# Layer 1's mixer in a two-layer encoder: values before keys and queries, the norm and the gates inside projection phases

## What is computed

```python
hn = rms_norm(x, mix_norm[layer])
u = hn @ od_w_in[j]
# mlstm_mixer(u, ...):
qk, v, o, gates = jnp.split(u, [ML_QK_W, ML_QK_W + D_MODEL, ML_QK_W + 2 * D_MODEL], axis=-1)
qk = jax.nn.silu(centered_dwconv(qk, conv_w, conv_b))
...
hs = mlstm_chunkwise(jnp.concatenate([q, flip(q)], axis=1), jnp.concatenate([k, flip(k)], axis=1),
                     jnp.concatenate([v, flip(v)], axis=1), log_i, log_f)
...
return hsum * jax.nn.sigmoid(o)
```

## Time and profile before

| | us |
|---|---|
| median of 3 runs | 2720.84 (2719.23 to 2721.32) |
| profiled execution, its time | 2724.51 |
| profiled execution, its span | 2722.5 |
| the five phases: renorm | 1411.4 to 1440.6 |
| ml_project_qk | to 1559.4 |
| ml_project_vo | to 1753.5 |
| ml_gates | to 1798.1 |
| ml_scan | to about 1911 |

### The profile page before, as it was taken

How to read it: one execution, slowest core, us unless ns; L and a number is a source line. 1 busy time by engine, 2 the same in 40 slices (tenths; PEclk the granted TensorE clock), 3 DMA queues, 4 the chain that set the end, 5 groups by cost and what they waited for, 6 DMA issues and landing times. The chain is left out here.

```text
span 2722.5 us, 32997 instructions
## 1 busy us (share of the span) xinstructions
PE 2428.2 (89%) x11788; PEld 1995.0 (73%) x11788; DVE 1827.1 (67%) x2083; ACT 1452.7 (53%) x1776; POOL 483.5 (18%) x433
## 2 busy tenths in 40 slices
PE   5989989796959999999948999779695999999995
PEld 4768877585857888888836888667584888888882
DVE  5748856578358998899835301078546988888980
ACT  4337842322227887788834212146423778887870
POOL 0001100100002332333200000025200323332310
PEclk9999999897979999999978999979796999999997
DMA  4010011101339999999980101200424999999994
GB/s 171 31 64 1 1 39 42 70 31 36 117 115 344 389 385 381 382 389 391 373 327 22 50 31 64 91 1 1 144 109 170 387 367 380 369 387 380 395 375 167
DMA packets 85787, 542.51 MB, mean 199 GB/s; under 512 B 18870, under 2 KB 22551, under 8 KB 59704
## 3 DMA queue, kind: packets, MB, share of 16 engines
q1 hardware_dynamic: 64232, 503.11, 47.0%
q0 software_dynamic: 19008, 33.61, 5.1%
q10 hardware_dynamic: 2448, 4.46, 0.4%
HBM read 521.70 MB, written 55.05 MB: 212 GB/s over the span
## 5 line engine op out<-in xcount | busy, mean ns | idle before, releaser
L2119 DVE TENSOR_TENSOR wL<-ring,wH 128x2048 fp32r<-128x2048 f32 x384 | 869.1, 2288 | 153.7 <-ACT wH L2066 148.4
L2066 ACT CAST wH<-ring 128x2048 fp32r<-128x2048 f32 x384 | 730.3, 1910 | 216.6 <-DMA ring<-in_moe_w 158.8
L1985 PE MATMUL psum<-wH,xgH 128*128 128x512 f32 x1024 | 408.0, 398 | 14.0 <-DVE xgL L2119 13.9
L1987 PE MATMUL psum<-wH,xgL 128*128 128x512 f32 x1024 | 401.3, 392 | 0.0
L1993 PE MATMUL psum<-wL,xgH 128*128 128x512 f32 x1024 | 275.4, 391 | 0.0
L1985 PEld LDWEIGHTS psum<-wH,xgH 128*128 128x128 f32 x1024 | 193.6, 189 | 57.3 <-DVE xgL L2119 13.0
L1993 PEld LDWEIGHTS psum<-wL,xgH 128*128 128x128 f32 x1024 | 193.0, 188 | 40.7
L1987 PEld LDWEIGHTS psum<-wH,xgL 128*128 128x128 f32 x1024 | 193.8, 189 | 38.4
L1985 PE MATMUL psum<-wH,hidH 128*128 128x512 f32 x512 | 207.8, 406 | 11.0 <-DVE hidL L2119 11.0
L1987 PE MATMUL psum<-wH,hidL 128*128 128x512 f32 x512 | 201.6, 394 | 0.0
L1932 POOL COPY gidx<-slots 128x1 int32 (+1 forms) x60 | 62.6, 1044 | 488.6 <-PE psum L2002 488.6
(11 more groups left out here) (425 smaller groups left out, 4728.9 us busy)
## 6 DMA issues: line engine op xcount, KB each, us to landing
ring<-in_moe_w SPq DMA_DIRECT2D x192, 2048.0 KB, 9.4
ring<-in_ev_w_in SPq DMA_DIRECT2D x6, 2048.0 KB, 14.7
xnT<-in_moe_w SPq DMA_DIRECT2D x6, 2048.0 KB, 13.8
ring<-in_od_w_in SPq DMA_DIRECT2D x6, 2048.0 KB, 15.4
xn_scratch<-xn_route SPq DMA_DIRECT2D x16, 512.0 KB, 2.6
ow<-in_moe_w SPq DMA_DIRECT2D x3, 2048.0 KB, 22.6
x_all<-in_x SPq DMA_DIRECT2D x4, 1024.0 KB, 8.1
ring<-in_ev_w_out SPq DMA_DIRECT2D x2, 2048.0 KB, 7.8
```

The costliest lines, as they stand in the source:

```text
L1985: nc.tensor.matmul(psum[:, bank, :], xh[:, k, :], w3[0][:, n, cols], start=(half == 0 and n == 0), stop=False)
L1987: nc.tensor.matmul(psum[:, bank, :], xl[:, k, :], w3[0][:, n, cols], start=False, stop=False)
L2066: nc.scalar.copy(half_of(wH, b, e, c, half), raw(e, c, half)).then_inc(w_high, 1)
L2119: return nc.vector.tensor_tensor(out, whole, high.bitcast(F32), ALU.subtract)
```

## The change

- `renorm` is gone. The new phase `ml_values` loads x tile by tile (three buffers), norms, turns, splits and at once uses it: both chunks of value weights are split once and kept, and for each tile PE makes 24 products with chunk 0, the 8 transposes of the next tile (`turn`), 24 products with chunk 1 and 24 gate products (`gates`), now with 16 moving columns in place of 144. Four copies spread them into `ml_G`, which is zeroed beforehand. ACT and DVE take the turned x straight from PSUM as xnH and xnL; xnT is no longer written in plain form.
- `ml_gates` now has the 16 groups of the output gates in it: the 32 row products come first, the computation on rows runs on DVE and ACT while PE projects, ACT's powers follow the sixth sigmoid, the 40 transposes follow group 7 (`turn_rows`) and the last two products group 9 (`finish`). The groups use four PSUM banks instead of eight.
- `ml_project_qk` comes last, without gates; the keys' four blocks come before the queries' and the convolution writes to its final place.
- The keys' 32 transposes stand at the head of `ml_scan`, with copies shared by ACT and DVE; the first scores wait for all of them.
- The chunks of `od_w_in` are loaded in the order of `ML_ORDER`.

The diff, cut:

```diff
+ML_ORDER = (2, 3, 4, 5, 1, 0)
...
-        @phase
-        def renorm(src, gain):
...
+        def ml_values(vA, xnH, G, src, gain):
...
+                        def load_x(j):
+                            if j < NT:
+                                if j >= 3:
+                                    sp.wait_ge(tr_hi, j - 2)
+                                sp.dma_start(x[:, j % 3, :], rows[:, j, :]).then_inc(x_in[j % 3], 16)
+                        load_x(0)
+                        sp.dma_start(g_bc[:], gain.partition_broadcast(P)).then_inc(gain_in, 16)
+                        load_x(1)
+                        load_x(2)
+                        sp.dma_start(gw[:], I["ml_gate_w"]).then_inc(gates_in, 16)
+                        for j in range(3, NT):
+                            load_x(j)
+                        for c in range(2):
+                            sp.wait_ge(proj, 2 * NT - 1 + c)
+                            load_chunk(sp, S_ML + c + RING)
...
+                        def turn(j):
+                            if j >= NT:
+                                return
+                            pe.wait_ge(xn_ok, j + 1)
+                            if j:
+                                pe.wait_ge(x_rest, 2 * j)
+                            for k in range(KD):
+                                last = nc.tensor.transpose(psum[:, XT + k // 4, (k % 4) * P:(k % 4 + 1) * P],
...
+                        def project(j, c):
+                            if j >= 2:
+                                pe.wait_ge(evac, 2 * j - 3 + c)
+                            for k in range(KD):
+                                if c == 0 and k % 4 == 0:
+                                    pe.wait_ge(x_rest, 2 * j + k // 4 + 1)
+                                if j == 0 and k % 2 == 0:
+                                    pe.wait_ge(w_rest, PARTS * c + k // 2 + 1)
+                                last = split_product(psum[:, 2 * (j % 2) + c, :], (xnH[:, k, tile(j)], xnL[:, k, tile(j)]),
+                                                     (wH[:, c, k, :], wide_rest(S_ML + c)[:, k, :]), k == 0, k == KD - 1)
                             last.then_inc(proj, 1)
...
+                        def gates(j):
...
+                                last = split_product(psum[:, GB, 16 * j:16 * j + 16], (xnH[:, k, tile(j)], xnL[:, k, tile(j)]),
+                                                     (gwH[:, k, :], gwL[:, k, :]), k == 0, k == KD - 1)
...
+                        turn(0)
                         for j in range(NT):
+                            project(j, 0)
+                            turn(j + 1)
+                            project(j, 1)
+                            gates(j)
...
                         split_w(0)
+                        square(0)
+                        split_w(1)
+                        root(0)
+                        split_w(2)
+                        split_w(3)
+                        split_x(0)
+                        square(1)
+                        split_w(4)
+                        root(1)
+                        split_w(5)
+                        split_w(6)
+                        split_w(7)
+                        act.wait_ge(gates_in, 16)
+                        nc.scalar.copy(gwH[:], gw[:]).then_inc(gate_high, 1)
+                        act.wait_ge(edges, 2)
+                        for j in range(NT):
+                            keep(j, 0)
+                            split_x(j + 1)
+                            square(j + 2)
+                            root(j + 2)
+                            keep(j, 1)
...
+                            at = n * GROWS + 32 * (n % 2)
+                            nc.scalar.copy(G[:, :, at:at + 4], made[:, :, n, :]).then_inc(spread, 1)
...
+        def ml_gates(xnH, G, cols, colb, apr):
...
+                        refill(sp, C0, C0 + CHUNKS, proj, NT)
...
+                        def turn_rows():
+                            pe.wait_ge(powered, 3)
+                            pe.wait_ge(ready, 1)
+                            for n in range(5 * NT):
+                                q, c = divmod(n, NT)
+                                row = (A, WI, ENM, KW, NEGM)[q]
...
+                        def finish():
+                            pe.wait_ge(moved, 3)
...
+                            if s >= 4:
+                                pe.wait_ge(evac, s - 3)
...
+                            if s == TURN:
+                                turn_rows()
+                            if s == TURN + 2:
+                                finish()
...
+                            nc.scalar.activation(so[:, b, :], psum[:, s % 4, :], ACT.Sigmoid).then_inc(evac, 1)
+                            act.wait_ge(evac, s + 1)
+                            act.dma_start(so_d[j * P:(j + 1) * P, c * HALF:(c + 1) * HALF], so[:, b, :]
+                                          ).then_inc(staged[b], 16)
+                            if s == POWERS:
+                                act.wait_ge(shifted, 2)
+                                nc.scalar.activation(ap[:], ap[:], ACT.Exp).then_inc(expd, 1)
+                                nc.scalar.activation(WI, WI, ACT.Exp).then_inc(powered, 1)
+                                nc.scalar.activation(ENM, ENM, ACT.Exp, scale=-1.0).then_inc(powered, 1)
+                                nc.scalar.activation(KW, KW, ACT.Exp).then_inc(powered, 1)
...
+                        split_w(0)
...
+                        split_w(1)
                         dve.wait_ge(turned, 1)
...
+        def ml_project_qk(qkT, xnH):
...
+                    return (i + 4) % CONV
...
+                            nc.scalar.activation(qkT[:, tile_of(i), :], qkT[:, tile_of(i), :], ACT.Silu).then_inc(silued, 1)
...
+                        for m in range(NT):
+                            if m >= 4:
+                                pe.wait_ge((k_lo, k_hi)[m % 2], m // 2 - 1)
+                            n = key_chunk(m)
+                            for h in range(MH):
+                                last = nc.tensor.transpose(psum[:, 4 + m % 4, h * P:(h + 1) * P],
+                                                           qkT[:, 4 + h, n * P:(n + 1) * P], ident[:])
+                            last.then_inc(k_turned, 1)
+                        pe.wait_ge(k_lo, NT // 2)
+                        pe.wait_ge(k_hi, NT // 2)
...
+                        for m in range(0, NT, 2):
+                            act.wait_ge(k_turned, m + 1)
+                            nc.scalar.copy(kn[:, key_chunk(m), :], psum[:, 4 + m % 4, :]).then_inc(k_lo, 1)
...
+                        pool_e.wait_ge(k_lo, NT // 2)
...
+                        for m in range(1, NT, 2):
+                            dve.wait_ge(k_turned, m + 1)
+                            V.tensor_copy(kn[:, key_chunk(m), :], psum[:, 4 + m % 4, :]).then_inc(k_hi, 1)
...
-            qkT = sb(ml, "ml_qkT", [P, 8, T])
...
+                ml_values(vA, xnH, G, xs, I["mix_norm"][1, :])
+                cols = sb(ml, "ml_cols", [P, 5, NT, GROWS])
+                colb = sb(ml, "ml_colb", [P, 5, NT, MH])
+                apr = sb(ml, "ml_decay", [P, NT, GROWS])
+                ml_gates(xnH, G, cols, colb, apr)
+                qkT = sb(ml, "ml_qkT", [P, 8, T])
+                ml_project_qk(qkT, xnH)
...
-    gw = np.zeros((D, 4, GROWS), np.float32)
+    gw = np.zeros((D, 4, 4), np.float32)
```

More of the change, by code:

```diff
@@ L2516, in _, with split_w @@
-                        silu(CONV - 1)
-                        for j in range(NT):
-                            act.wait_ge(proj, CONV + j + 1)
-                            nc.scalar.copy(G[:, j, :], psum[:, j, 0:4 * GROWS]).then_inc(evac, 1)
+                        def split_w(n):
+                            c = n // PARTS
+                            if n % PARTS == 0:
+                                chunk_wait(act, S_ML + c)
+                            nc.scalar.copy(wH[:, c, part(n), :], wide(S_ML + c)[:, part(n), :]).then_inc(w_high, 1)
@@ new lines, in split_x, with keep @@
+                        def split_x(j):
+                            if j >= NT:
+                                return
+                            for half, ready in ((0, tr_lo), (1, tr_hi)):
+                                act.wait_ge(ready, j + 1)
+                                nc.scalar.copy(xnH[:, quad(half), tile(j)], turned(half)).then_inc(x_high, 1)
+                        def keep(j, c):
+                            act.wait_ge(proj, 2 * j + c + 1)
+                            nc.scalar.copy(vA[:, j, 2 * c:2 * c + 2, 0:MV],
+                                           psum[:, 2 * (j % 2) + c, :].rearrange("p (h e) -> p h e", h=2)).then_inc(evac, 1)
@@ L2556, in ml_project_qk @@
+                        V.memset(vA[:, :, :, MV:MVA], 1.0).then_inc(edges, 1)
+                        V.memset(G[:], 0.0).then_inc(edges, 1)
+                        for j in range(NT):
+                            split_x(j + 1)
```

(12 more changed lines are left out.)

505 lines of the change are left out of this document (222 added, 283 removed).

## The result

The changed kernel takes 2686.41 us (median of 4 runs, 2681.64 to 2691.58) against 2721.08 beside it: a ratio of 0.9872, with a 95% interval of 0.9856 to 0.9888, or 34.7 us less. The prediction was 2691.1, or 29.7 us less. The profiled execution took 2691.58 us with a span of 2689.8, against 2722.5 before, so 32.7 of it is seen in the trace. From the start of the mixer's first phase to the scan's first scores it is 386.7 us before (1411.4 to 1798.13) and 355.0 after (1411.3 to 1766.28): 31.8 us are gained there. From the scan's first scores to the end of the span it is 924.4 us before and 923.5 after.

The account below looks back on a forecast made before the run. TensorE, busy for 89% of the span, was taken as the bound, with four holes in layer 1's mixer. Terms 23.9 - 7.7 + 0 + 1.1 + 29.5 - 2.4 - 7.0 - 7.7 = 29.7 us off 2720.84 gave 2691.1; range 2679 to 2708.

Parts of the forecast that it names:

- head: Start of the mixer, where x is normed, turned and split: the first product comes earlier, gaining 23.9 us.
- turns: Values' phase: seven tiles' transposes now stand between products, 1.10 us per tile, losing 7.7 us.
- gate products: Values' phase: 192 products with 16 instead of 144 moving columns still take 21.6 us, paced by operand loads; change 0.
- clock slips: Values' phase: low-clock starts of large products after gate products; the forecast charged nothing, leaving them to rival 1.
- values to output gates: Boundary between value products and row products: 2.2 us without TensorE work instead of 3.3, gaining 1.1 us.
- gates' phase: The gates' computation on rows, hidden behind output gate products: of 44.6 us, 15.1 stay, gaining 29.5 us.
- stores, barrier, split: After the last sigmoid: store and barrier stay at 10.0 us, the key weights' first split adds 2.4 us of loss.
- end of keys and queries: After the last query product: copy, convolution and silu of 5.8 us plus a 1.2 us barrier lie uncovered, losing 7.0.
- keys' transposes: Head of the scan: 32 transposes at the low clock, 6.85 us, plus last copy and signals, losing 7.7 us.
- rival 3: Values' phase: gate products get cheap, priced by moving columns; some 16 us more gained, 2675 us; chance 0.09.
- rival 2: Values' phase: clock falls within the gate products themselves; eight stretches lose 4.7 each, 37.6 us, giving 2728.7; chance 0.04.
- rival 1: Values' phase: clock slips after narrow gate products and turns; eight slips of 2.0, 16 us, giving 2707.1; chance 0.09.

Follow-up runs that it names:

- rows_exposed: Changed kernel with the 40 row transposes and last two products before the first output gate, ACT's powers right after its logarithm: 2716.13 us, ratio 0.9981.
- gates_last: Changed kernel with all gate products, still 16 moving columns, together at the end of the values' phase: 2695.29 us, ratio 0.9898.
- gates_last_wide: gates_last with the 16 columns taken eight times, 128 moving columns, at the same place: 2679.91 us, ratio 0.9845.

## Why the prediction was right, and where its terms were off

The terms as predicted, and as the profile of the changed kernel has them, in us gained:

| term | predicted | measured | from |
|---|---|---|---|
| head | 23.9 | 23.65 | first product at 1423.15 for 1446.8 |
| turns | -7.7 | -6.2 | 7 x (0.79 + 0.09) |
| gate products | 0 | +0.5 | 8 x (2.59 + 0.09) for 21.9 |
| clock slips | 0 | -6.4 | 4 x 1.6 |
| values to output gates | 1.1 | 1.6 | 1.7 for 3.3 |
| gates' phase | 29.5 | 30.5 | 8.7 + 2.7 + 1.05 + 1.6 left of 44.6 |
| stores, barrier, split | -2.4 | -0.4 | 10.4 for 10.0 |
| end of keys and queries | -7.0 | -6.7 | |
| keys' transposes | -7.7 | -7.5 | 1758.79 to 1766.28 |
| sum | 29.7 | 29.1 | 31.8 in the local time |

The 2.7 us that the measured terms leave over are in the 1152 large products themselves: without their low-clock starts they take about 267.5 us before (180.8 and 90.7, each with one start of 2.0) and 265.4 after (values 88.3, output gates 88.9, keys and queries 88.2), and the two starts themselves were 0.6 shorter. No experiment was made for that. The median gained 34.7 us, 2.9 more than the local time; what that is stays open.

**Right, and for its reason.** The two large gains were read rightly: both holes were chains over DVE and ACT with nothing for TensorE, and both went behind products. The head is off by 0.3 us. The wait for the gain vector, which the prediction gave up to 2 us, was 0.7 of DVE's time ahead of its first scaling. The rows' gain is what rows_exposed takes back, with a wait of 24.89 us for the 24.8 of the sum. The two ends that the new order uncovers cost 6.7 and 7.5 for 7.0 and 7.7.

**Wrong in one step: "0" for the gate products.** Their own price was right, and rival 3 (a price by the moving columns) was false: 0.11 us each with 16, 128 or 144 columns. But the argument against a slipping clock, 21.6 us of gate products at 1.00, was drawn from products with 144 columns, and at one and the same place the clock held with 128 columns and fell with 16. gates_last shows how far it could have gone: in a long stretch the clock fell within the gate products, as rival 2 has it. Of rival 1, the eight slips of 2.0 became four of 1.6. The Trainium skill, page "TensorE: Matmul & The Clock Gate", section "HAM oscillation — how this bites in real kernels", lays such oscillation on waits between bursts of products. Here the clock fell with no wait at all, TensorE busy for 124.25 of 124.30 us. The prediction's own marks caught it: PEclk in the values' phase is 0.93, under the 0.95 that was named.

**Mis-sized, and made up for the slips.** A turn between products costs 0.88, not 1.10: its tail of 0.24 us lies under the next product. The 40 row transposes cost 2.7, not 4.45, being placed among products at the upper level, though in this execution 1.6 of that came back as a low start after them. The last store landed in 6.3 us, not 8.2, so that the hole with the first split of the key weights came to 10.4, not 12.4; the split itself cost its 2.35 (ACT's cast starts at 1659.99, the product at 1662.34). These three are 1.5 + 0.1 + 2.0 = 3.6 of the 6.4 that the slips cost; with the boundary (0.5), the row products (0.7) and the packing of the products (2.7) the sum came out 2 us too small rather than 6 too large. The right total is in part luck.

**Not foreseen.** ACT loads a table (1.28 us at 1767.67) for the scan's first exponential, since silu is now its last function before; it stands beside the first unit, and the scan is no longer than before: 111.9 us from its first scores to the last addition on POOL, for 112.4.

## What to carry to other kernels

A hole that is a chain over slow engines goes whole if its input comes early and its output is wanted late: then look at what the new order uncovers, here 14 us of convolution tail and transposes that used to have cover, because moved work that was free in one place isn't in the next. Price narrow products by the load of the stationary operand where the trace shows that load busy throughout, but look at the clock in a row with the same moving columns: here narrow products that cost nothing themselves slowed the wide ones after them by 6.3 us, and widening them, or mixing them in, cost nothing. And when two orders differ by a few us, read the stretch that the edit touches in the profile beside the median, as the rest of the program may spread by more; then take that stretch apart too, lest a low start that one execution happens to have be counted as a gain.

## What the runs showed of the hardware

- With products of 16 moving columns back to back, TensorE's clock fell from 2.4 to 1.2 GHz while the engine was busy throughout and its operand loads ran for 35.05 of 35.10 us; with 128 columns at the same place it stayed at 1.00 (gates_last against gates_last_wide, 38.0 against 21.4 us for 192 products).
- After 24 such products (2.6 us) the fall came with delay, in the wide products 0.4 to 1.3 us later, and after three or four of the seven stretches that have wide products behind them (six profiles).
- With 128x128 stationary operands narrow products came every 0.11 us at the upper clock, with 16, 128 and 144 moving columns alike, and every 0.21 at the lower with 16.
- Transposes that directly followed products ran at the upper clock: 40 of 36x36 in 2.7 us against 4.45 after a wait, 16 of 128x128 in 1.9 against 3.67.
- A 256 KB store issued beside a 2 MB load took 6.3 us to land instead of 2.0, and 8.2 in the kernel before.
